# Expert weights loaded in halves, and products that wait for one half of their operand, in a two-block transformer kernel on one core

## The reference

```python
def hybrid_layer(x, ...):                      # twice
    z = rms_norm(x, g_mix_pre) @ w_in
    y = concat(retention(z), dilated_attention(z), spatial_gating(z))
    x = x + rms_norm(y @ w_out, g_mix_post)
    gate, up = split(rms_norm(x, g_ffn_pre) @ w_gate_up)
    return x + rms_norm((silu(gate) * up) @ w_down, g_ffn_post)
def second_block(x, ...):                      # once
    merged = g_a * (ssd(x) @ w_branch_a) + g_p * (pool(x) @ w_branch_b)
    x = layer_norm(ALPHA * x + mod * (merged @ w_out))
    y = hier_moe(x)      # 32 experts of 1024 x 512 x 3 weights, 2 of them for each token
    return layer_norm(ALPHA * x + mod * y)
```

## Time and profile before

| | |
|---|---|
| profiled execution, device time | 1652.5 us |
| its span | 1650.7 us |
| median of 3 runs | 1652.82 us |
| busy: PE, DVE, ACT, POOL | 1588.2, 764.5, 613.7, 476.8 us |
| mean granted TensorE clock | 0.993 |
| DMA, mean over the span | 397.87 MB, 241 GB/s |
| chain that ended last | PE 82%, DMA 9%, DVE 4% |

### The profile page before, as it was taken

How to read it: one execution, slowest core, us unless ns; L and a number is a source line. 1 busy time by engine, 2 the same in 40 slices (tenths; PEclk the granted TensorE clock), 3 DMA queues, 4 the chain that set the end, 5 groups by cost and what they waited for, 6 DMA issues and landing times.

```text
span 1650.7 us, 24318 instructions
## 1 busy us (share of the span) xinstructions
PE 1588.2 (96%) x9881; PEld 1208.0 (73%) x9881; DVE 764.5 (46%) x1263; ACT 613.7 (37%) x1115; POOL 476.8 (29%) x305
## 2 busy tenths in 40 slices
PE   6999999999999999999999999999999999999996
PEld 5988999869879998888778888898644444444442
DVE  4544433246463332478776666446533333333223
ACT  4643444345544443554456555333211111111111
POOL 4332654433334444300036555343300000000000
PEclk9999999999999999999999999999999999999998
DMA  7644997546429996333323333956899999999994
GB/s 262 221 148 127 252 271 233 173 140 214 152 72 296 264 264 227 124 83 102 97 57 103 103 102 118 297 148 244 355 416 422 426 420 423 423 422 424 421 422 174
DMA packets 244261, 397.87 MB, mean 241 GB/s; under 512 B 6725, under 2 KB 195585, under 8 KB 223280
## 3 DMA queue, kind: packets, MB, share of 16 engines
q1 hardware_dynamic: 237360, 365.45, 63.9%
q10 hardware_dynamic: 3760, 20.85, 3.2%
q0 software_dynamic: 3024, 9.95, 1.8%
HBM read 395.17 MB, written 1.05 MB: 240 GB/s over the span
## 4 chain that ended last, share of the span: by engine, by line
PE 82%; DMA 9%; DVE 4%; POOL 2%; ACT 2%; issue 2%; ACTq 0%; DVEq 0%; POOLq 0%; SPq 0%
PE ps L145 80%; DMA arena<-in_w_expert_up 4%; DMA ring<-in_w_expert_gate 4%; PE ps L147 2%; DVE arena L155 1%; DVE split_r L151 1%; ACT arena L149 1%; DVE arena L151 1%; POOL split_r L151 1%; POOL stat L151 1%; DMA X<-in_x 1%; ACT split_r L149 1%; POOL arena_r L151 0%; DMA ring<-in_w_out 0%; DVE X L155 0%
## 5 line engine op out<-in xcount | busy, mean ns | idle before, releaser
L145 PE MATMUL ps<-arena_r,split_r 128*128 128x256 f32 (+1 forms) x2984 | 461.5, 289 | 3.8 <-POOL split_r L151 3.8
L151 POOL TENSOR_TENSOR split_r<-ring,split_r 128x1024 fp32r<-128x1024 f32 (+1 forms) x142 | 334.3, 2355 | 302.7 <-ACT split_r L149 265.0
L145 PEld LDWEIGHTS ps<-arena_r,split_r 128*128 128x128 f32 x2984 | 394.8, 189 | 21.3 <-issue 16.1
L149 ACT ACTIVATE split_r<-ring 128x1024 fp32r<-128x1024 f32 (+1 forms) x293 | 296.4, 1019 | 268.0 <-PE ps L145 200.5
L151 DVE TENSOR_TENSOR split_r<-ring,split_r 128x1024 fp32r<-128x1024 f32 (+1 forms) x151 | 217.3, 1442 | 309.2 <-ACT split_r L149 309.0
L145 PE MATMUL ps<-split_r,arena_r 128*128 128x512 f32 (+1 forms) x1520 | 341.0, 378 | 2.4 <-issue 1.7
L145 PEld LDWEIGHTS ps<-split_r,arena_r 128*128 128x128 f32 x1520 | 276.0, 189 | 48.7 <-issue 5.4
L145 PE MATMUL ps<-arena 128*64 128x512 f32 (+8 forms) x1448 | 297.0, 462 | 12.0 <-DMA arena<-in_w_expert_up 4.2
L145 PEld LDWEIGHTS ps<-arena 128*64 128x64 f32 (+2 forms) x1448 | 125.5, 148 | 134.4 <-issue 118.0
L145 PE MATMUL ps<-hhh_r,split_r 128*128 128x256 f32 (+1 forms) x976 | 221.7, 316 | 0.0
L145 PE MATMUL ps<-ring,arena 128*64 128x512 f32 (+2 forms) x768 | 211.7, 576 | 6.5 <-DVE arena L151 2.3
(11 more groups left out here) (164 smaller groups left out, 1238.4 us busy)
## 6 DMA issues: line engine op xcount, KB each, us to landing
ring<-in_w_gate_up SPq DMA_DIRECT2D x88, 512.0 KB, 7.5
arena<-in_w_expert_up SPq DMA_DIRECT2D x15, 2048.0 KB, 28.8
arena<-in_w_expert_gate SPq DMA_DIRECT2D x15, 2048.0 KB, 28.4
ring<-in_w_expert_down SPq DMA_DIRECT2D x15, 2048.0 KB, 30.1
ring<-in_w_in SPq DMA_DIRECT2D x57, 512.0 KB, 5.3
ring<-in_w_expert_gate SPq DMA_DIRECT2D x13, 2048.0 KB, 26.3
arena<-in_w_ada SPq DMA_DIRECT2D x24, 1024.0 KB, 7.3
ring<-in_w_down SPq DMA_DIRECT2D x22, 1024.0 KB, 5.0
```

The lines of the kernel that those rows point to most:

```text
L145: made = e.matmul(*a, **k)
L149: made = e.activation(*a, **k)
L151: made = e.tensor_tensor(*a, **k)
```

## The change

1. **Halves of a norm.** The z products wait for half q of `HTR` at k = 4q. `gates_raw(i)` takes both units in turn for each half: unit 0's four steps, unit 1's four steps, then the other half. Unit 0 is free only near the end of it.
2. **DVE's order.** In three places (gates of both layers, z of layer 1) `norm_scaled` of tile 1 moves ahead of `lo_to`.
3. **The third load** goes out in two halves of 1 MB from ACT in turns u = 2 and 3.
4. **Loads 9, 10 and 92 to 95** go in halves. `("gu", 0, 0, "first")` marks the end of four of the eight steps of pair 0's gate product: then the first halves of loads 9 and 10 go, the second halves behind the whole product. For 92 to 95 the order is half 0 of two experts, half 1 of both, all issued when the later one's place is free. PE waits for a half at k = 4 (up), or after two of four steps (down, last pair, both column halves h in turn).
5. **The end.** The last pair's result is put back by one product in full precision with `PLACE`, in place of two rounded ones each; `OEH` and `OEL` of that pair go. The `sums` move: two into the up product of pair 15 between its halves, two around the transposes. `variance` of tile 0 stands ahead of the last `bn_stats`, and the final operations are in another order, with the same number.

```diff
+        in_halves = lambda r, k: r == 0 and (k in (2, 9, 10) or k >= 92)
+
+        def half_load(e, k, q):
+
+            p, j = divmod(k, 6)
+            o = slot_for(0, k)[:, q * RAW:(q + 1) * RAW]
+            w = A["w_expert_up_2" if j < 4 else "w_expert_down_2"][0, 2 * p + j % 2]
+            src = w.rearrange("(q p k) n -> q p (k n)", q=2, k=4)[q] if j < 4 else w.rearrange("(p q k) n -> q p (k n)", q=2, k=2)[q]
+            e.dma_start(o, src).then_inc(*landed(s_second[k % 4] if q else s_w[0][k % 9], ("ew", 0, k, q)))
...
-                    for q in range(2):
-                        t.wait_ge(*at("hr", j, i, q))
                     for k in range(8):
                         if k % 4 == 0:
+                            t.wait_ge(*at("hr", j, i, k // 4))
                             t.wait_ge(*at("raw", u0 + k // 4))
                         made = t.matmul(bk[:, 0:384], HTR[:, k, tok(i)], fold(raw_of(u0 + k // 4)[:, 0:1536], 4)[:, k % 4, :], k == 0, k == 7)
...
-                def gate_up_raw(m, i):
-                    u = first["up", l, m][0]
-                    t.wait_ge(*at("raw", u))
+                def gates_raw(i):
+
                     for a in range(2):
-                        x = fold(raw_of(u)[:, a * 1024:(a + 1) * 1024], 8)
-                        made = summed(B("up", l, m)[:, 256 * a + i * P:256 * a + (i + 1) * P], [(x[:, k, :], HTR[:, k, tok(i)]) for k in range(8)])
-                    return made
+                        for q in range(2):
+                            t.wait_ge(*at("hr", j + 1, i, q))
+                            for m in range(2):
+                                u = first["up", l, m][0]
+                                t.wait_ge(*at("raw", u))
+                                x = fold(raw_of(u)[:, a * 1024:(a + 1) * 1024], 8)
+                                for k in range(4 * q, 4 * q + 4):
+                                    made = t.matmul(B("up", l, m)[:, 256 * a + i * P:256 * a + (i + 1) * P], x[:, k, :], HTR[:, k, tok(i)], k == 0, k == 7)
+                                if a and q and i:
+                                    made.then_inc(*sig(s_mm, ("up", l, m), ("free", u)))
...
+                            if k == 4 and p == 15 and part:
+                                for x in range(2):
+                                    sums(0, x)
                             if k % 4 == 0:
+                                weights_in(k0, k // 4)
                                 t.wait_ge(*at("hg", r, p, k // 4, "kept"))
                             t.matmul(bk[0:64, :], HG[:, i, k, 0:64], wa[:, k, :], k == 0, k == 7)
                             made = t.matmul(bk[64:128, :], HG[:, i, k, 64:128], wb[:, k, :], k == 0, k == 7)
+                            if r == 0 and p == 0 and part == 0 and k == 3:
+                                made.then_inc(*sig(s_done, ("gu", 0, 0, "first")))
...
+                        take(("oe", r, p, h), ("oe", r, p, h, "kept"), hold=True)
+                    for q in range(2):
+                        weights_in(k0, q)
+                        for h in range(2):
+                            for k in (2 * q, 2 * q + 1):
+                                made = product(h, k)
+                            if q:
+                                made.then_inc(*sig(s_done, ("oe", r, p, h)))
+                    for h in range(2):
+                        drop(("oe", r, p, h))
...
-                    t.wait_ge(*at("oeh", r, 15, h))
-                    t.wait_ge(*at("oel", r, 15, h))
+                    t.wait_ge(*at("oe", r, 15, h, "kept"))
                     for x in range(2):
-                        bk = B("ya", r, 15, h, x)
-                        t.matmul(bk, ONET[:, 1, tok(x)], OEH[:, half(h)], False, False)
-                        t.matmul(bk, ONET[:, 1, tok(x)], OEL[:, half(h)], False, True).then_inc(*sig(s_done, ("ya", r, 15, h, x)))
+                        t.matmul(B("ya", r, 15, h, x), PLACE[:, tok(x)], OE[:, 0, half(h)], False, True).then_inc(*sig(s_done, ("ya", r, 15, h, x)))
...
-                    if u == 0:
+                    if u >= 2:
                         s.wait_ge(*at("ba", 3))
-                        expert_load(s, 0, 2)
+                        half_load(s, 2, u - 2)
...
+                norm_scaled(j + 1, 1)
                 lo_to(first["up", l, 2][1] + 4)
-                norm_scaled(j + 1, 1)
...
-                    if k >= n_slots:
+                    if k >= n_slots and not (r == 0 and k in (9, 10)):
                         b, i = divmod(k - n_slots, 6)
                         y.wait_ge(*(at("gu", r, b, i // 2) if i < 4 else at("oe", r, b, 1)))
-                    expert_load(y, r, k)
+                    if not in_halves(r, k):
+                        expert_load(y, r, k)
+                    elif k == 10:
+                        for q in range(2):
+                            y.wait_ge(*at("gu", 0, 0, 0 if q else "first"))
+                            for x in (9, 10):
+                                half_load(y, x, q)
...
+                    elif k % 2 and k > 90:
+                        for q in range(2):
+                            for x in (k - 1, k):
+                                half_load(y, x, q)
```

More of the change, by code:

```diff
@@ L373, in program @@
         s_w = [[sem(f"expert{i}") for i in range(9)]] + [[sem(f"expert{r}_{i}") for i in range(8)] for r in range(1, ROUNDS)]
+        s_second = [sem(f"expert_second{i}") for i in range(4)]
         s_round = [None] + [{e: sem(f"round{r}_{e}") for e in ("pe", "act", "dve")} for r in range(1, ROUNDS)]
@@ L1330, in experts @@
                     else:
-                        sums(0, 0)
+                        sums(1, 0)
                     turn_products(p)
@@ L1336, in experts @@
                     else:
-                        sums(0, 1)
+                        sums(1, 1)
                     down(p)
                 combine_last(0)
-                for x in range(2):
-                    sums(1, x)
                 combine_last(1)
@@ L1815, in experts @@
                         gather(p + 1)
-                    for h in range(2):
+                    for h in range(2 if p < 15 else 0):
                         s.wait_ge(*at("oe", r, p, h, "kept"))
@@ L2552, in last_norm @@
                     v.wait_ge(*at("ln_row", 2, k))
[L2553 to L2557 removed]
+                halves = [(0, 0), (0, 1), (1, 0), (1, 1)]
+                for i, h in halves:
+                    if name == 2:
+                        v.wait_ge(*at("full", 0, h, i))
+                    v.stt(OE[:, i, half(h)], YA[:, i, half(h)], MV[:, i, 0:1], GB[:, 0, half(h)], ALU.subtract, ALU.mult).then_inc(*sig(s_done))
+                    if i == 0:
+                        continue
+                    v.wait_ge(*at("rstd", name, 0))
+                    v.wait_ge(*v.latest)
+                    v.stt(OE[:, 0, half(h)], OE[:, 0, half(h)], RV[:, 0:1], GB[:, 1, half(h)], ALU.mult, ALU.add).then_inc(*sig(s_done, ("ln", name, 0, h)))
+                v.wait_ge(*v.latest)
+                for i, h in halves[2:]:
                     v.wait_ge(*at("rstd", name, i))
[L2559 to L2561 removed]
+                    v.stt(OE[:, i, half(h)], OE[:, i, half(h)], RV[:, i:i + 1], GB[:, 1, half(h)], ALU.mult, ALU.add).then_inc(*sig(s_done, ("ln", name, i, h)))
             def experts(r, s_done):
@@ L2643, in experts @@
                         then(v.bn_stats(BN[:, x, h, :], B("ya", r, 15, h, x)), ("ya", r, 15, h, x, "kept"))
-                if r == 0:
-                    for x in range(2):
-                        variance(2, x, s_done)
+                        if r == 0 and h:
+                            variance(2, x, s_done)
             then(v.memset(negh[:, :], -0.5), ("neg",))
@@ L2978, in store @@
             def store(name, s_done):
-                for i in range(2):
-                    for h in range(2):
-                        y.wait_ge(*at("ln", name, i, h))
-                        y.dma_start(out[0][tok(i), half(h)], OE[:, i, half(h)]).then_inc(*landed(s_done, ("out", name, i, h)))
+                for i, h in ((0, 0), (0, 1), (1, 0), (1, 1)):
+                    y.wait_ge(*at("ln", name, i, h))
+                    y.dma_start(out[0][tok(i), half(h)], OE[:, i, half(h)]).then_inc(*landed(s_done, ("out", name, i, h)))
             store(2, s_out[0])
```

49 lines of the change are left out of this document (21 added, 28 removed).

## The result

The changed kernel takes **1639.93 us** (median of 5 runs, 1638.58 to 1642.94), where the kernel before took 1652.82 beside it (5 runs as well). The ratio is 0.9916, with a 95% interval of 0.9898 to 0.9933: 11 to 17 us less. The forecast was 1636.8, with a range of 1632.0 to 1643.5. The profiled execution took 1638.58 us, its span is 1636.8 us, 13.9 less than the span before.

A forecast was written before the change was run, and what follows sets the result against it. The prediction took full DMA engines (422 GB/s) to bound the expert stage and PE the time before it. Terms 3.5 + 0.8 + 2.55 + 4.2 + 1.0 + 3.7 = 15.75 us, from 1652.5, gave 1636.8 us, range 1632 to 1643.5.

The forecast's parts named there:

- Raw products of layer 1: Layer 1's z stage: both waits of PE go, second raw products start at 359.55 instead of 363.07; 3.5 us.
- Gates of layer 0: Layer 0's gates: waits of 1.28 and 1.32 us go, but late weights leave 0.8 us; bounds -0.3 and 2.55.
- Gates of layer 1: Layer 1's gates: 2.55 us of waits go and fit into the 4.1 us of room before GpSimd's low part is needed.
- Third load: Second branch: without this load ahead, its last weights land sooner, removing PE's 2.56 us idle and 1.64 more; 4.2 us.
- The rival by which its parts hold up w_out: At w_out: the third load's two halves add 3.0 us to each of two transfers; +6.0 us, 1642.8; chance 0.08.
- First two places: Start of the expert weight stream: first halves start 3.5 us sooner, of which 1.0 us remains; bounds 0 and 3.5.
- the hole of load 13: Expert stream: load k = 13 waits for pair 0's down product, so the stream can run dry again; 1.0 of 3.5 us remains.
- Last pair: Kernel's end: down product 3.2 us sooner, final operations start at 1637.1 instead of 1640.82; 3.7 us, bounds 2.5 and 5.5.
- The first one: Rival, both layers: weights late wherever PE comes sooner; gates give nothing, z stage only 1.25; 10.15 us, 1642.3; chance 0.10.
- cut loads each cost their own latency: Rival, weight stream: six more transfers at 2.6 us each cost 15.6 us, so 1652.4, no change; chance 0.03.
- The fixed cost: DMA transfers: about 2.0 us each by the Trainium skill, which would speak against cutting loads; the prediction took it as overlapped.

## Why the prediction was right, and where it failed

- **Raw products of layer 1, 3.5 us: the step that failed.** Its own working was right (PE's second product 3.8 us earlier, both waits gone), but the forecast stopped there. It said of the gates of layer 0 "then weights are late next", and did not ask that of the z stage: DVE's splits, moved behind the scaling, release SyncE's ring load, and POOL's table is not held back by them. The load lost its place to the table, and 3.1 of 3.8 us were returned by waiting. The version with the table behind the loads shows it: it gets 3.1 us back. The clock took 1.6 us more in this stage and gave 1.55 back at 454 us; that is in no part of the working, and only by luck does it leave the sum alone.
- **Gates of layer 0, 0.8 us: too low, 1.85.** The way was right. POOL's two splits took 4.68 us against 6.69, as worked out (4.8), and PE waits for POOL at the fifth unit. By the rule of the Trainium skill ("SBUF — State Buffer", "Who interferes with whom") the value was 0.8; the trace agrees with it in those durations, and with DVE's old order they are 4.52 and 6.71 us again. But DVE's two took 3.13 us from 147.73, so that the low part was there 0.75 us sooner, and the fifth unit's two transfers, issued 0.4 us sooner, landed after 6.9 and 8.3 us where they took 8.2 and 9.6: 1.7 us sooner. That shorter landing wasn't in the working, and no run shows what makes it. The stage gives 1.4 to 1.9 us in the traces that have it as in the change, and 1.1 in the one with DVE's old order: 0.3 to 0.8 us of it are DVE's order.
- **Gates of layer 1, 2.55: 2.75.** Kept to the end; 1.2 of it is DVE's order.
- **Third load, 4.2: 4.05** by the comparison of traces, 3.8 by the version with the early load. The 1.64 of the working beside the wait of 2.56 is the lower clock of the trace before (its stretch begins at 1129.7 us); it is not there each time, since behind 2.28 us in the version with the early load the clock stayed at 1.00. The rival by which its parts hold up w_out has 0.64 us in the change, not 6.0: the transfers behind the halves land after 6.6, 5.6 and 5.7 us, not after the 7.9 of the working.
- **First two places, 1.0: 0.7 and 1.1.** The size was taken from the hole of load 13. That hole is there (1.4 us, and the load takes 7.9 us, forecast 7.6), but there is one more of 1.2 us at load 11, which the working did not have. The mechanism was right and one of its two places was missing.
- **Last pair, 3.7: 3.5**, 3.1 ahead of the down product (forecast 3.2) and 0.4 behind it (0.5). The 8.78 us of the up product before are again the lower clock behind a wait. What PLACE, the moved sums and the order of the final operations are worth each is not shown; no version takes them back one by one.

The sum of the measured parts is 13.9 us, that of the spans; the medians give 12.9. Against 15.75 the shortfall is 1.85: the table's 3.1 us (the 4.7 of the list of stages, less the 1.55 of the clock), less the 1.1 that layer 0's gates gave more; the rest cancels to 0.2. No rival with its mechanism came true. The first one named the right kind of loss (a layer gives it back to its loads), but put it in the gates as well, where both layers kept theirs. That cut loads each cost their own latency is answered by the stream: 422 GB/s before and after, with six more transfers in it. The fixed cost that the prediction names beside that rival stands in the Trainium skill ("DMA: Bandwidth & Descriptors", "Anatomy of one DMA — SWDGE (gpsimd) path") for transfers of GpSimd; the loads cut here are ACT's and SyncE's.

## What to carry to other kernels

Where an engine's work is moved ahead or behind, ask of each queue that it releases whether another queue's transfer now goes first; a load that nobody awaits belongs behind the ones that someone does. Halves of the last loads pay where work stands ready between them, and the work moved there costs if they don't come. A wait removed in a stage is worth what is left of it at the end of that stage, so read the start of the next stage's first product in both traces, not the wait, and the granted clock between the two places with it.

## What was not expected of the hardware

Single executions of the change lie as far apart as 1637.52 and 1644.53 us, and part of that is the clock behind a wait. Windows of PE in three versions near w_out's last products and the tokens' transposes (us, PE busy, clock, DMA share, GB/s); first the change, where PE waited 1.33 us until 1141.95 and its clock stayed at 1.00:

```profile
1164.00:1166.00 2.00, 1.55 (x7) 0.50 1.02 428
```

the version with the later table, where PE waited 2.56 us until 1140.01:

```profile
1140.00:1142.00 2.00, 1.99 (x5) 0.54 1.05 446
1142.00:1144.00 2.00, 2.00 (x7) 0.61 1.05 446
```

and the one with the early third load, which idled as much behind w_out (1.77 and 0.93 us, where the other two have 1.76 and 0.45, and 1.76 and 0.93):

```profile
1166.00:1168.00 2.00, 1.16 (x10) 1.00 1.01 420
```

The clock stands at 2.4 GHz (1.00) or at 1.2 (0.50). After 1.33 us of waiting at w_out it stayed, after 2.56 it fell (0.54 and 0.61 in two windows of 2 us) and w_out's last 36 products took 10.21 us instead of 8.68; behind the later waits of the same stage it fell in two of the versions and stayed in the third.

The length of the wait alone doesn't decide it. Behind the same wait of 1.02 us near 450 us it fell in five of the fourteen traces, the one before among them, and stayed in the others, the change's among them. Behind the waits in z of layer 1 it fell in four of the nine traces that have this stage as in the change. Behind 2.28 us in the version with the early load it stayed. Each such stretch costs PE some 1.6 us. So the profile of the version with the later table, 3.2 us ahead at 1054 us, was 1.7 behind at the first expert product, and took 1640.23 us where its median is 1636.22. A gain ahead of such a place is read in front of it, and a median over several executions decides.
